# VectorE's order in a hybrid decoder step: weight halves around the mask, keys behind the maximum, prompt scores a group ahead

## The reference, cut to what matters

```python
h = rmsnorm(x, norm_g);  proj = h @ w_in          # q, keys, values, gates, za, u, v, zb, r
s = einsum('bqgjd,bcgd->bgjqc', q, kc)            # compressed keys
p = masked_softmax(s, cend <= qpos);  imp = p @ overlap
idx = top_k(where(forced, BIG, where(valid, imp, NEG)), 16)   # blocks to attend to
p_sel = masked_softmax(q . kg, msel);  p_win = masked_softmax(q . kw, mw)
o = g0 * o_cmp + g1 * (p_sel @ vg) + g2 * (p_win @ vw)
pa = (o * silu(za)) @ w_pa;  pb = (sgu * silu(zb)) @ w_pb
y = rmsnorm(x + (sigmoid(ra) * pa + sigmoid(rb) * pb) @ w_o)
```

## Time and profile before

| | |
|---|---|
| time, median of 3 runs | 537.23 us (536.1 to 539.24) |
| profiled execution: own time | 538.56 us |
| profiled execution: span | 536.8 us |
| around the span | 1.76 us |
| TensorE busy | 518.6 us, 97% of the span |
| VectorE busy | 330.9 us, 62% |
| ScalarE busy | 243.0 us, 45% |
| GpSimd busy | 157.3 us, 29% |
| mean granted clock of TensorE | 0.999 |

### The profile page before, as it was taken

One profiled execution on the slowest core, in us unless ns is written; L12 is line 12 of the kernel. 1 busy time (PEld: TensorE's weight loads), 2 busy tenths in 40 slices (PEclk: granted clock), 3 DMA queues, 4 the chain that ended last, 5 costly groups with the idle time before them and its releaser, 6 DMA issues.

```text
span 536.8 us, 12832 instructions
## 1 busy us (share of the span) xinstructions
PE 518.6 (97%) x5198; PEld 473.0 (88%) x5198; DVE 330.9 (62%) x838; ACT 243.0 (45%) x564; POOL 157.3 (29%) x257
## 2 busy tenths in 40 slices
PE   6899999999999999999989999999999999999995
PEld 4899999999999999986988776777779999999995
DVE  5723231388798775575565679687762467763565
ACT  6543424534533323241241787687773532323334
POOL 0006933044513644644000074573453000000000
PEclk9999999999999999999999999999999999999999
DMA  8527652447526464877331266573554534306104
GB/s 301 213 83 220 233 186 81 156 135 263 197 74 195 137 202 141 263 287 226 129 101 58 58 157 186 140 187 76 156 144 119 155 100 150 117 1 198 42 6 162
DMA packets 59790, 81.05 MB, mean 151 GB/s; under 512 B 7826, under 2 KB 49234, under 8 KB 59219
## 3 DMA queue, kind: packets, MB, share of 16 engines
q1 hardware_dynamic: 48320, 49.97, 29.8%
q0 software_dynamic: 10688, 29.14, 17.9%
q10 hardware_dynamic: 722, 1.12, 0.6%
HBM read 65.23 MB, written 8.13 MB: 137 GB/s over the span
## 4 chain that ended last, share of the span: by engine, by line
PE 85%; DVE 5%; ACT 4%; issue 3%; DMA 1%; POOL 1%; DVEq 0%
PE m L1744 58%; PE so L1915 3%; PE so L1918 3%; PE so L1916 3%; PE so L2054 3%; PE so L2045 2%; PE m L1828 2%; DVE p_turn L1650 2%; PE so L1954 2%; PE so L1892 1%; ACT U L1235 1%; PE so L2003 1%; PE t L1880 1%; PE t L1770 1%; DVE U L1626 1%
## 5 line engine op out<-in xcount | busy, mean ns | idle before, releaser
L1744 PE MATMUL m<-h_hi,w_hi 128*128 128x272 f32 x448 | 132.4, 296 | 1.0 <-DVE za L1441 0.8
L1744 PE MATMUL m<-h_hi,w_lo 128*128 128x272 f32 x448 | 129.2, 288 | 0.0
L1744 PE MATMUL m<-h_lo,w_hi 128*128 128x272 f32 x448 | 128.7, 287 | 0.0
L1744 PE MATMUL m<-w_hi,h_hi 128*128 128x256 f32 (+2 forms) x360 | 103.9, 289 | 2.4 <-issue 1.8
L1744 PE MATMUL m<-w_lo,h_hi 128*128 128x256 f32 (+2 forms) x360 | 101.6, 282 | 0.0
L1744 PE MATMUL m<-w_hi,h_lo 128*128 128x256 f32 (+2 forms) x360 | 101.6, 282 | 0.0
L1328 DVE TENSOR_TENSOR w_lo<-raw,w_hi 128x1024 fp32r<-128x1024 f32 (+2 forms) x62 | 71.0, 1155 | 43.2 <-ACT w_hi L1061 39.3
L1744 PEld LDWEIGHTS m<-h_hi,w_hi 128*128 128x128 f32 x448 | 84.2, 188 | 11.2 <-issue 7.9
L1017 POOL DMA_DIRECT2D U<-p_turn x108 | 58.4, 548 | 99.3 <-DVE p_turn L1650 97.9
L1744 PEld LDWEIGHTS m<-h_lo,w_hi 128*128 128x128 f32 x448 | 84.5, 189 | 0.0
L1744 PEld LDWEIGHTS m<-h_hi,w_lo 128*128 128x128 f32 x448 | 84.5, 189 | 0.0
(11 more groups left out here) (304 smaller groups left out, 915.2 us busy)
## 6 DMA issues: line engine op xcount, KB each, us to landing
raw<-in_w_in SPq DMA_DIRECT2D x36, 512.0 KB
U<-in_x_p SPq DMA_DIRECT2D x8, 512.0 KB, 5.7
raw<-in_w_o SPq DMA_DIRECT2D x8, 512.0 KB
U<-p_turn POOLq DMA_DIRECT2D x54, 64.0 KB, 2.6
U<-p_turn SPq DMA_DIRECT2D x42, 64.0 KB, 2.8
raw<-in_w_in SPq DMA_DIRECT2D x8, 256.0 KB
raw<-in_w_pa SPq DMA_DIRECT2D x8, 256.0 KB
raw<-in_w_pb SPq DMA_DIRECT2D x4, 512.0 KB
```

What stands on the lines that cost most here:

```text
L1744: ins = mm(out, lhs(a, k), rhs(b, k), start=(k == 0 and a + b == 0), stop=(k == n - 1 and a == 1))
```

## The change

Only `plan()` changes, and with it the order; no step is added or removed.

1. **Keys behind the maximum.** Keys 0 and 1 of group 1 are turned behind `s_max` of group 0 (before: behind `s_turn`, with key 2), keys 2 to 5 behind `s_turn` (before: 3 to 5 behind `s_imp`).
2. **Weight halves around the mask.** Both low halves of ZB0 (group 0) and of RA0 (group 1) stood right ahead of `s_mask`, behind a tile. Now the first stands ahead of that tile and the second behind the tile that follows `s_mask`.
3. **The prompt's scores a group ahead.** `("cs", 0)` moves from behind the second tile after group 1's exponentials to right behind `s_exp`, ahead of `s_scale` and both tiles.
4. **The second turn a unit later.** `("ct", k, 1)` moves from the end of unit 4k, behind its products, into unit 4k+1, behind that unit's first tile.

```diff
@@ -307,13 +307,13 @@
             order += [(step, q)]
-            if q == 0 and n in (1, 2):
-                keys(1, 3 * n - 3, 3)
+            if q == 0 and n < 2:
+                keys(1, 2 * n, 2 * n + 2)
             if step == "s_exp":
+                if q == NQ - 1:
+                    order += [("cs", 0)]
                 order += [("s_scale", q)]
                 main(1)
-                if q == NQ - 1:
-                    order += [("cs", 0)]
             main(1)
@@ -328,8 +328,12 @@
     for q, name in enumerate(("ZB0", "RA0")):
-        order.remove(("low", SLOT[name], 1))
-        order.insert(order.index(("s_mask", q)), ("low", SLOT[name], 1))
+        for hf in range(2):
+            order.remove(("low", SLOT[name], hf))
+        at = order.index(("s_mask", q))
+        before, behind = max(n for n in range(at) if order[n][0] == "main"), min(n for n in range(at, len(order)) if order[n][0] == "main")
+        order.insert(behind + 1, ("low", SLOT[name], 1))
+        order.insert(before, ("low", SLOT[name], 0))
@@ -353,8 +357,8 @@
-        if n == 0:
-            order += [("ct", k, 0)]
+        if n < 2:
+            order += [("ct", k, n)]
@@ -365,8 +369,6 @@
-        if n == 0:
-            order += [("ct", k, 1)]
```

## The result

The changed kernel takes 531.69 us (median of 4 runs, 531.66 to 533.61), the kernel before on the same chip 537.78 us (4 runs, 536.1 to 539.24): a ratio of 0.9908, 95% interval 0.9885 to 0.993. Six more runs on another chip gave 532.64 us against 536.7: 0.9925, 0.9903 to 0.9948. So the gain is 6.1 us in the first comparison and 4.1 us in the second. The forecast was 533.1 us, range 531.3 to 536.2, and a gain of 4.1 us.

What follows compares the result with a forecast made beforehand. TensorE's matmuls were taken as the bound, busy 518.6 of 536.8 us, so only its waits could be won: 1.2 + 1.5 + 0.9 + 0.5 = 4.1 us, giving 533.1 us, range 531.3 to 536.2.

Steps and rivals of the forecast that it cites:

- Group 0: In decode: tile 51's wait goes (0.94 us, plus 0.1 for the slower restart) and the turn comes 0.2 us sooner: 1.2 us.
- The margin at tile 51: In group 0: the second weight half ends 0.2 us before TensorE would come to tile 51.
- The open price: In group 0: whether keys 4 and 5 land in time; a small, hidden stall assumed, up to 2.6 us paid at worst.
- Group 1: In decode: tile 59's wait 0.2 us, the turn 0.2 us and the wait for L1593 1.1 us go: 1.5 us.
- Block 0: At its second turn: scores 1.4 us sooner, less 0.4 for transposes and 0.1 for ScalarE's copy: 0.9 us gained.
- block 1: At its second turn: the wait of 0.41 us goes and ScalarE has over 2 us to copy: 0.5 us gained.
- Blocks 2 and 3: At their second turns: no wait to remove, and the moved transposes cost what they save: 0.
- The waits for moves: At about 395 us: the moves hang on a turn of TensorE that shifts along, so the earlier gain is kept.
- Keys late: Rival, group 0: VectorE stands 2 to 3.6 us at key 4 or 5; gain about 2.3 us, 534.9 us; chance 0.12.
- no change: Rival: the wait for moves at about 395 us takes everything back; 537.2 us; chance 0.05.
- slower: Rival, blocks 0 to 2: TensorE waits for ScalarE's copy; from 2.3 us each, 2.7 us or more slower, 540 us; chance 0.07.
- the unit loop keeps what decode does not give: Rival, 298 to 331 us: TensorE waits for VectorE's masks, losing the turns' 0.9 and 0.5; gain 2.7, 534.5 us; chance 0.14.

## Why the prediction was right

Its cause holds, and so does its sum: 4.1 us were forecast, and between executions without the stand and without waits for moves the stages give 23.80 - 22.72 = 1.1 in group 0, 0.74 + 1.17 = 1.9 in group 1, 0.6 and 0.6 in blocks 0 and 1, and 0.2 in blocks 2 and 3: 4.3 to 4.4 us, by how one rounds. That the sum comes so near is in part luck: its terms miss by -0.3 to +0.4 us and partly cancel. Step by step:

- **Group 0: 1.2 forecast, 1.1 measured** (1.3 against the execution of the earlier trace rows, whose tile 51 waited 0.24 us longer than in the other profile of before). The margin at tile 51 was 0.35 us for a forecast of 0.2. It takes parts 1 and 2 together: keys alone give 0, halves alone 0.35.
- **The open price** was as the medians had it (at most 0.8 us, hidden by the slack): key 4, issued at 221.51, was there at 225.55, 4.0 us later, the median of the earlier trace rows, and VectorE's 0.73 us stall, for 0.8 us in hand, put off tile 48's eviction by 0.2 us and TensorE by nothing. By the estimate of 2.6 us from the Trainium skill ("DMA: Bandwidth & Descriptors", section "Anatomy of one DMA — SWDGE (gpsimd) path") it would have landed at 224.1, before VectorE came to it at 224.8; the trace, with 4.0 us, does not agree. With all keys early a price shows: 3.7 us, of which 1.4 is the lower clock behind the stand; the prediction's worst, 2.6 us, left that out.
- **Group 1: 1.5 forecast, 1.9 measured.** The mechanism is right, the term mis-sized: tile 59's wait was taken as 0.2 us from the waits, which count idle time as the brackets do, and start to start it is 0.53 - 0.09 = 0.44; the turn was taken as 0.2 us with a usual step of 0.2, and is 0.42 - 0.12 = 0.30. The prediction counts from start to start at tile 51 and does not do so at tile 59. It also credited the wait for L1593 to part 3; each of parts 2 and 3 removes it alone, and together they remove it once.
- **Block 0: 0.9 forecast, 0.6 measured; block 1: 0.5 and 0.6.** ScalarE's copy holds `("cs", 1)` by 0.12 us, for 0.1 forecast. In block 0 the cost was short: the slower step behind a moved turn (0.09) was left out, and the scores up to block 0's `cv` take 0.2 us more.
- **Blocks 2 and 3: 0 forecast, 0.2 measured**: a turn directly behind a tile costs a little less than at the unit's end.
- **The waits for moves** were taken to shift along unchanged; they vary from 0 to 1.4 us with the execution.

The parts' own gains add up: 0 for part 1, 0.35 + 1.92 for part 2, 1.2 for part 3, 1.4 for part 4 make 4.8; less 1.17 that parts 2 and 3 share, plus 0.73 in group 0 that neither part 1 nor part 2 gives alone, it is 4.4.

The predicted time lies 1.4 us above the first median and 0.5 above the second. Some 0.2 us of it is the sum and 0.4 to 0.5 the base: before's medians over 65 further runs were 536.7 to 536.84, not 537.23. What is left of the first is chance as far as the runs show: three of the four first runs of after lie at 531.66 to 531.72, and the six later ones spread from 531.56 to 533.83. That this median lies within the range is luck too: decode's 2.7 us at half as much again would put the lower end near 531.8, and the prediction puts it at 531.3. The profiled execution of before held the 1.74 us stand; going from it to the median by the difference of the two (1.33) let most of that fall out of the forecast without its having been seen.

**The rivals.** Keys late, no change and slower did not come. Of "the unit loop keeps what decode does not give" only this came: block 0 gave a third less than forecast. Decode's gains went through whole. Two of the signs that the prediction lists as wrong did come, both small: VectorE's gap of 0.73 us ahead of key 4, which TensorE did not feel, and the prompt's scores behind ScalarE's copy, 0.12 us.

## What to carry to other kernels

Where TensorE is busy 97% of the span and still waits, look for what stands ahead in the queue of the engine that it waits for: two weight halves, moved around a mask, gave 2.3 of the 4.3 to 4.4 us here by themselves. Price a wait from start to start, not by the idle time in brackets, and ask of each wait whether another part of the change removes it already. One execution holds stands that are its own: a second profile of the same program, or any variant whose program is unchanged up to that stretch, tells them from the kernel's.

## What was not expected of the hardware

A wait can cost more than its length. Behind the 2.48 us stand in group 0 (all keys behind the maximum) TensorE's granted clock was at its lower level until about 228.6 us and cost 1.4 us more; behind the stands of 0.8 to 1.25 us at tiles and turns in the other profiles, the matmuls step by 0.125 us again within two of them. It need not come each time: the lower clock followed the stand of some 2 us ahead of 19 us in three of fourteen profiles, with the same program up to there. And TensorE stood once for 1.04 us within group 1's scores with nothing in the trace that it waited for; its cause stays open.
